# Early issue of expert weight pieces, and the first expert's gather made by channels in four parts, in a hybrid SSD, attention and mixture-of-experts layer

## The chip, the cores and the metric

One core of a Trainium2 chip runs the whole layer as one program, written engine by engine with semaphores. The metric is the device time of one execution in microseconds (us); the median of three runs is given before.

## What is computed

One decoder layer on 256 tokens of width 1024, in f32: a norm, one wide projection, a state space branch and a causal attention branch with forget gates, their gated merge; a cross attention to a memory of 256 rows; and a mixture of 32 experts, of which each token takes 4. All matrices are read from memory once. Cut to the part that the change is in:

```python
# h = h + cross_attention(...), 256 tokens x 1024
u = rms_norm(h, norm_ffn_g)
logits = u @ w_router + b_router                 # 32 experts
top_vals, top_idx = lax.top_k(logits, 4)
gates = softmax(top_vals)
# for each expert e, on the tokens x that chose it:
hgl = x @ w1[e] + b1[e]                          # 1024 -> 2048, 8 MiB of weights
glu = minimum(hgl[:, :1024], 7.0)
lin = clip(hgl[:, 1024:], -7.0, 7.0)
act = glu * sigmoid(1.702 * glu) * (lin + 1.0)
out[tokens] += gate * (act @ w2[e] + b2[e])      # 1024 -> 1024, 4 MiB of weights
```

## The kernel before

**The first half, to about 424 us,** is dense projections. Weights come in units of 256 columns (1 MiB each), which SP loads in the order of a list into two buffers (`load(u)`, L383). ScalarE rounds each to a high part (`w_hi`, L1205), VectorE makes the low part (`w_lo`, L1565), and TensorE makes three products of each (L648 to L650). The last units are `ck` and `cv` (keys and values of the cross attention), `cq`, and `co` (its output projection, `in_w_cross_o`). `load(u)` waits until the unit two before is split (L385).

**The experts, from 434.8 us,** use each expert's 12 MiB once. The working memory is an arena of 25 pages of 8 KiB per partition. Eleven slots of two pages each hold expert weights; a half piece `m` is 2 MiB, three pairs of them make an expert: two pairs of `w1`, by input channels, and one of `w2`. The first eleven halves go to slots that are still used by the first half's tensors (`W_AT`, L188): slot 3 lies on pages 6 and 7 (`kxT` and `Vx`, keys and values of the cross attention), slot 8 on pages 18 and 19 (the split memory rows, `B_`), slot 9 on pages 20 and 21 (`qx`, then squares). So SP brings them in quarters of 1 MiB, `piece(m, k)` (L388), each placed by hand in SP's order behind a wait for the tensor that it overwrites (L411 to L446). Halves 11 and 12 follow in quarters when the first expert's first products have been made (`first_page`, L458), and from 13 on each half waits for the release of the half that was in its slot (`e_free`, L346; L464 and L470). From the eighth expert to the thirtieth, both halves are loaded as one 4 MiB transfer (`whole`, L366).

SP has one instruction stream: a wait in it holds all that stands behind. TensorE, ScalarE, VectorE likewise run the order in which the code is written.

**The routing, 424 to 435 us.** TensorE makes the last logits and square sums, then turns `hT` (channels by tokens) to tokens by channels in PSUM with products by the identity (`by_token`, L862), and ScalarE copies four tiles of 128x512 to `xtok`, scaled by the token's norm (`tokens`, L1414). VectorE picks the four largest logits of each token and makes the mask `msk` (L1834). TensorE sums the mask over the tokens before each one (L918 to L920: a token's place in its expert's list) and counts each expert's tokens (L921, L922). VectorE makes from this `posm`, and from it the selection matrix `sel` of the first expert (`selection`, L1838: token by slot, 64 slots) and the counts of further items (L1863, L1864). `keep_clock` (L888) is one product of 128x256 of constants into an unused bank, once before these products and once behind them.

**The first expert's gather:** TensorE multiplies `sel` by `xtok`, all 1024 channels, the two halves of them side by side in the two halves of bank 2 (`gather(1)`, L955), 64 columns of weights and 512 moving ones. ScalarE copies the result in two parts (L1436), TensorE transposes it in four (`gathered_transposes`, L964), and VectorE scales it by the gains of the norm and writes `xgT`, channels by slots (L1868), in two parts. `weights_in` (L999) then multiplies `xgT`, 64 columns of weights at a time, by the expert's `w1`: four parts `(s, h)`, of half a piece each, in 16 instructions. Every later expert's gather and transposes are made while the one before it is at work (`item`, L1070), in the same way.

```python
gather(1)                       # waits for tok_ready 4: all four token tiles
offsets()                       # places of further items
bias(0); bias(1)
gathered_transposes(1)
```

## Time and profile before

| | |
|---|---|
| runs | 1341.42 us median of 3 (1339.36 to 1342.38) |
| the profiled execution | 1341.73 us, of which the span from first to last instruction is 1340.0 us |
| TensorE (PE) busy | 1295.9 us, 97% |
| VectorE (DVE) busy | 423.0 us, 32% |
| ScalarE (ACT) busy | 326.0 us, 24% |
| moved by DMA | 474.79 MB, 354 GB/s over the span |
| granted TensorE clock, mean | 0.989 |

The profile is one execution. Its views used here: the busy shares and the memory rate in 40 slices; the same by stretches (windows); who waited for whom (waits); the chain of work that ended last, followed back (chain); instructions in order of time (timeline); the DMA issues with their time from issue to landing; groups of instructions by line. An f32 product that is not a plain transpose shows as two instructions. PEld is TensorE's weight load, SPq the DMA issues of SP. Neighbouring instructions of one kind are merged: the second number is then the length of the group.

### The profile page before, as it was taken

To read this page: it belongs to the slowest core of one execution; us is meant where nothing else is said; L and a number is where in the kernel's file an instruction comes from. 1 tells how busy PE (TensorE), PEld (TensorE's weight loads), DVE (VectorE), ACT (ScalarE), POOL (GpSimd) and SP (SyncE) were. 2 spreads that over 40 slices of the span, in tenths; PEclk is the share of its full clock that TensorE was granted. 3 is DMA by queue.
4 is the path that set the end of the run, shared out by engine and by line. 5 is a ranking of instruction groups with operands and counts; after the bars stand their busy time and mean duration, and the time that the engine had idled before them with its cause. 6 is when DMAs were issued, how large, how long until landed. Compare 5 with 4: busy or idle time off the path is not lost.

```text
span 1340.0 us, 17338 instructions
## 1 busy us (share of the span) xinstructions
PE 1295.9 (97%) x7372; PEld 717.8 (54%) x7372; DVE 423.0 (32%) x803; ACT 326.0 (24%) x533; POOL 39.8 (3%) x66
## 2 busy tenths in 40 slices
PE   8999999999999999999999999999999999999997
PEld 7999999999998333333333333333333333333332
DVE  6765777586453212111121112111112111112111
ACT  5865456554443111000010001000001000000102
POOL 2002210001001000000000000000000000000000
PEclk9999999999999999999999999999999999999999
DMA  7566544559839999999999999999999999999996
GB/s 225 163 205 205 160 141 141 160 187 368 292 119 409 389 429 427 417 435 428 435 430 428 433 429 435 428 433 432 429 435 427 435 430 431 435 427 433 426 425 252
DMA packets 88930, 474.79 MB, mean 354 GB/s; under 512 B 7398, under 2 KB 68998, under 8 KB 70568
## 3 DMA queue, kind: packets, MB, share of 16 engines
q1 hardware_dynamic: 88176, 470.71, 86.6%
q10 hardware_dynamic: 696, 3.24, 0.7%
q8 instruction: 45, 0.74, 0.2%
q14 instruction: 13, 0.11, 0.0%
HBM read 472.86 MB, written 1.07 MB: 354 GB/s over the span
## 4 chain that ended last, share of the span: by engine, by line
PE 70%; DMA 24%; DVE 3%; ACT 1%; issue 0%; ACTq 0%; DVEq 0%
DMA arena<-in_w_expert_in 23%; PE ps L1014 21%; PE ps L1066 13%; PE ps L648 6%; PE ps L650 6%; PE ps L649 6%; PE ps L980 4%; PE ps L960 3%; DVE w_lo L1565 1%; PE ps L972 1%; PE ps L988 1%; DMA w_raw<-in_w_in 1%; PE ps L639 1%; PE ps L1042 1%; PE ps L640 1%; PE ps L641 1%
## 5 line engine op out<-in xcount | busy, mean ns | idle before, releaser
L1014 PE MATMUL ps<-arena 128*64 128x512 f32 x2048 | 462.1, 607 | 25.4 <-DMA arena<-in_w_expert_in 24.9
L1014 PEld LDWEIGHTS ps<-arena 128*64 128x64 f32 x2048 | 148.3, 140 | 331.5 <-issue 290.7
L1907 DVE TENSOR_SCALAR arena<-ps 128x512 f32<-128x512 f32 x32 | 22.1, 692 | 664.8 <-PE ps L1014 664.8
L1066 PE MATMUL ps<-arena 128*64 128x512 f32 x1024 | 227.0, 595 | 0.0
L648 PE MATMUL ps<-A_hi,w_hi 128*128 128x256 f32 x576 | 165.5, 287 | 2.9 <-DVE w_lo L1565 2.2
L1565 DVE TENSOR_TENSOR w_lo<-w_raw,w_hi 128x1024 fp32r<-128x1024 f32 x120 | 145.1, 1250 | 66.8 <-ACT w_hi L1205 66.5
L649 PE MATMUL ps<-A_lo,w_hi 128*128 128x256 f32 x576 | 162.9, 283 | 0.0
L650 PE MATMUL ps<-A_hi,w_lo 128*128 128x256 f32 x576 | 162.9, 283 | 0.0
L1066 PEld LDWEIGHTS ps<-arena 128*64 128x64 f32 x1024 | 70.6, 137 | 135.6 <-issue 135.5
L1442 ACT ACTIVATE arena<-arena 128x512 f32<-128x512 f32 x32 | 20.1, 629 | 479.0 <-DVE arena L1907 479.0
L1205 ACT ACTIVATE w_hi<-w_raw 128x1024 fp32r<-128x1024 f32 x120 | 120.1, 1048 | 36.6 <-DMA w_raw<-in_w_cross_o 6.8
L648 PEld LDWEIGHTS ps<-A_hi,w_hi 128*128 128x128 f32 x576 | 110.4, 192 | 5.4 <-issue 3.6
L649 PEld LDWEIGHTS ps<-A_lo,w_hi 128*128 128x128 f32 x576 | 110.4, 192 | 0.1
L650 PEld LDWEIGHTS ps<-A_hi,w_lo 128*128 128x128 f32 x576 | 110.4, 192 | 0.0
L1454 ACT ACTIVATE arena<-ps 128x512 f32<-128x512 f32 x32 | 19.1, 597 | 236.5 <-PE ps L1066 236.5
L980 PE MATMUL ps<-arena 64*128 64x512 f32 x264 | 65.6, 615 | 0.7 <-ACT arena L1454 0.7
L960 PE MATMUL ps<-arena,wrt 128*64 128x512 f32 x256 | 62.0, 605 | 0.1
L980 PEld LDWEIGHTS ps<-arena 64*128 64x128 f32 x264 | 22.7, 186 | 43.1 <-issue 41.5
L1849 DVE TENSOR_TENSOR arena<-ps,prm 128x512 f32<-128x512 f32 x31 | 21.4, 692 | 70.8 <-PE ps L972 70.8
L960 PEld LDWEIGHTS ps<-arena,wrt 128*64 128x64 f32 x256 | 15.5, 136 | 42.2 <-issue 41.8
L1432 ACT ACTIVATE arena<-ps 128x512 f32<-128x512 f32 x31 | 18.5, 597 | 75.3 <-PE ps L960 75.3
L648 PE MATMUL ps<-C_hi,w_hi 128*128 128x256 f32 x128 | 36.3, 284 | 0.4 <-DVE w_lo L1565 0.4
(309 smaller groups left out, 1274.8 us busy)
## 6 DMA issues: line engine op xcount, KB each, us to landing
arena<-in_w_expert_in SPq DMA_DIRECT2D x46, 4096.0 KB, 37.4
arena<-in_w_expert_out SPq DMA_DIRECT2D x23, 4096.0 KB, 39.4
arena<-in_w_expert_in SPq DMA_DIRECT2D x27, 2048.0 KB, 17.2
w_raw<-in_w_in SPq DMA_DIRECT2D x32, 1024.0 KB, 5.4
arena<-in_w_expert_out SPq DMA_DIRECT2D x10, 2048.0 KB, 15.1
arena<-in_w_expert_in SPq DMA_DIRECT2D x18, 1024.0 KB, 10.5
arena<-in_w_expert_out SPq DMA_DIRECT2D x16, 1024.0 KB, 20.8
w_raw<-in_w_cross_kv SPq DMA_DIRECT2D x8, 1024.0 KB, 7.6
```

Source lines behind the costliest of these rows:

```text
L648: mm(o, w_hi[:, s, k, :], a_hi[:, k, :], start=(k == 0), stop=False)
L649: mm(o, w_hi[:, s, k, :], a_lo[:, k, :], start=False, stop=False)
L650: last = mm(o, w_lo[:, s, k, :], a_hi[:, k, :], start=False, stop=(k == KT - 1))
L960: last = mm(ps[64 * half:64 * (half + 1), 2, :], sel[:, 64 * tb:64 * (tb + 1)], xtok[:, tb, 512 * half:512 * (half + 1)], start=(tb == 0), ...
L980: last = mm(ps[:, 4 + 2 * tb + half, :], sgT[rows, tb * P:(tb + 1) * P], ys[rows, :], start=False, stop=bool(each), skip_group_check=True)
L1014: last = mm(ps[64 * half:64 * (half + 1), b, :], xg_cols[:, 2 * h + c, s, :], columns[:, :, half, :], start=False, stop=(s + h + c == 3), ...
L1066: last = mm(ps[64 * half:64 * (half + 1), bank, :], cols[:, c, h, :], w[:, at:at + 512], start=(h + c == 0), stop=(h + c == 4))
L1205: A(w_hi[:, p % 4, :, :], raw_w[u % 2][:, :, j * P:(j + 1) * P], ACT.Copy).then_inc(w_hi_ready, 1)
L1442: A(sig, glu, ACT.Sigmoid, scale=ALPHA).then_inc(sig_ready, 1)
L1565: V_.tensor_tensor(w_lo[:, p % 4, :, :], raw_w[u % 2][:, :, j * P:(j + 1) * P], w_hi[:, p % 4, :, :].bitcast(f32), ALU.subtract).then_inc( ...
L1849: V_.tensor_tensor(xgT.rearrange("p (m a j) -> p m a j", m=4, a=2), ps[:, 2, :].rearrange("p (m a j) -> p m a j", m=4, a=2), prm[:, 136:14 ...
L1907: V_.tensor_scalar(glu, ps[:, 0, :], LIMIT, None, ALU.min).then_inc(glu_ready, 1)
```

## The change

Three edits.

1. SP's order. Quarter (9,0) (page 20, `qx`) and (3,0) (page 6, `kxT`) are issued as soon as the last scores of the cross attention are made (`x_psum`), then, when the last value projection is done (`w_done`), (8,0), the third `co` load, (8,1), the fourth `co` load; only (3,1) (page 7, `Vx`) still waits for the attention's outputs (`xo_psum`).
2. `keep_clock` and its two products are gone.
3. The first expert's gather is made by channels: `first_gather(part)` has the token tile (every fourth of 512 channels, 128 of them) as weights and `sel` as the moving operand, so that channels by slots come out directly, 2 groups of 128 channels a part. The copy on ScalarE and the transposes are gone for the first expert. VectorE scales each of the four parts by itself. Parts 0 and 1 are made before the bias, parts 2 and 3 between the first products of `weights_in`, as are the offsets. ScalarE copies the token tiles of the first 512 channels first. The semaphores' counts move with it.

```diff
--- before.py
+++ after.py
@@ -424,14 +424,16 @@
             piece(4, 1)
             for u in range(unit("cv", 3), unit("co", 2)):
                 load(u)
+            sp_.wait_ge(x_psum, X_H)
+            piece(9, 0)
+            piece(3, 0)
+            sp_.wait_ge(w_done, 2 * unit("cv", 3) + 2)
+            piece(8, 0)
+            load(unit("co", 2))
+            piece(8, 1)
+            load(unit("co", 3))
             sp_.wait_ge(xo_psum, X_H)
-            load(unit("co", 2))
-            piece(3, 0)
-            load(unit("co", 3))
             piece(3, 1)
-            piece(9, 0)
-            for k in range(2):
-                piece(8, k)
             sp_.wait_ge(w_lo_ready, 2 * (NU - 1))
             piece(6, 0)
             sp_.wait_ge(w_lo_ready, 2 * NU)
@@ -885,11 +887,6 @@
                 pe.wait_ge(dve_drained, drained(unit("co", 2))[1])
                 logits(2)
 
-            def keep_clock(bank, n):
-
-                for _ in range(n):
-                    mm(ps[:, bank, 0:S], idn, tri[:, 0:S], start=True, stop=True)
-
             def square_sums(chunks):
 
                 for c in chunks:
@@ -913,14 +910,12 @@
             square_sums((6, 7)).then_inc(ms_psum, 1)
             for c in range(2, 8):
                 by_token(c)
-            keep_clock(2, 1)
             pe.wait_ge(msk_ready, 1)
             mm(ps[:, 0, 0:NE], tri[:, 0:P], msk[:, 0, :], start=True, stop=True)
             mm(ps[:, 0, NE:2 * NE], tri[:, P:2 * P], msk[:, 0, :], start=True, stop=False)
             mm(ps[:, 0, NE:2 * NE], tri[:, 0:P], msk[:, 1, :], start=False, stop=True).then_inc(pos_psum, 1)
             mm(ps[0:NE, 3, 0:1], msk[:, 0, :], tri[:, P:P + 1], start=True, stop=False)
             mm(ps[0:NE, 3, 0:1], msk[:, 1, :], tri[:, P:P + 1], start=False, stop=True).then_inc(cnt_psum, 1)
-            keep_clock(2, 1)
 
             def offsets():
 
@@ -961,15 +956,20 @@
                                   xtok[:, tb, 512 * half:512 * (half + 1)], start=(tb == 0), stop=(tb == TB - 1))
                 last.then_inc(xg_psum, 1)
 
+            def first_gather(part):
+
+                s, h = part // 2, part % 2
+                for m in (2 * h, 2 * h + 1):
+                    at = 2 * P + SLOTS * (m % 2)
+                    for tb in range(TB):
+                        last = mm(ps[:, 2 + h, at:at + SLOTS], xtok[:, tb, 512 * s + m:512 * (s + 1):4],
+                                  sel[:, 64 * tb:64 * (tb + 1)], start=(tb == 0), stop=(tb == TB - 1))
+                last.then_inc(xgt_psum, 1)
+
             def gathered_transposes(i1):
-                first = type(i1) is int and i1 == 1
-                pe.wait_ge(xg_copied, i1 + (0 if first else 1))
+                pe.wait_ge(xg_copied, i1 - 1)
                 for m in range(4):
-                    if first and m == 2:
-                        last.then_inc(xgt_psum, 1)
-                        pe.wait_ge(xg_copied, 2)
-                    bank, at = (3, 2 * P + m * P) if first and m < 2 else (2, m * P)
-                    last = nc.tensor.transpose(ps[:, bank, at:at + P], xgs[:, m:512:4], idn)
+                    last = nc.tensor.transpose(ps[:, 2, m * P:(m + 1) * P], xgs[:, m:512:4], idn)
                 last.then_inc(xgt_psum, 1)
 
             def scatter(each=None):
@@ -987,23 +987,25 @@
 
                 mm(ps[:, b, :], selb[:, :], b1p[:, b, :], start=True, stop=False, skip_group_check=True)
 
-            pe.wait_ge(tok_ready, 4)
-            gather(1)
-            offsets()
+            pe.wait_ge(sel_ready, 2)
+            pe.wait_ge(tok_ready, 2)
+            first_gather(0)
+            pe.wait_ge(extra_ready, 1)
+            first_gather(1)
             pe.wait_ge(b1_ready, 2)
             pe.wait_ge(selb_ready, 1)
             for b in range(2):
                 bias(b)
-            gathered_transposes(1)
 
             def weights_in(i, parts):
 
                 first = type(i) is int and i == 0
-                pe.wait_ge(xgt_ready, i + (1 if first else 2))
+                if not first:
+                    pe.wait_ge(xgt_ready, i + 4)
                 for s in range(2):
                     for h in range(2):
-                        if first and (s, h) == (0, 1):
-                            pe.wait_ge(xgt_ready, 2)
+                        if first:
+                            pe.wait_ge(xgt_ready, 2 * s + h + 1)
                         w, loaded = parts[2 * s + h]
                         if loaded:
                             pe.wait_ge(*loaded)
@@ -1016,6 +1018,11 @@
                             if type(i) is int and (i, s, c) == (0, 0, 0):
                                 last.then_inc(first_page, 1)
                         last.then_inc(h_psum if s + h == 2 else e_used, 1)
+                        if first and s == 0:
+                            pe.wait_ge(tok_ready, 4)
+                            if h:
+                                offsets()
+                            first_gather(2 + h)
                         if type(i) is int and i == TABLES_AT:
                             if (s, h) == (0, 1):
                                 pe.wait_ge(y_ready, i + 1)
@@ -1411,9 +1418,10 @@
                 pair_square("co", n)
             root(3)
 
-            def tokens(tb):
-                for half in range(2):
-                    act.wait_ge(tok_psum, 2 * half + 2)
+            def tokens(half):
+
+                for tb in range(TB):
+                    act.wait_ge(tok_psum, 4 if half or tb else 2)
                     A(xtok[:, tb, 512 * half:512 * (half + 1)], ps[:, 4 + 2 * tb + half, :], ACT.Copy,
                       scale=st[:, tb:tb + 1]).then_inc(tok_ready, 1)
 
@@ -1424,16 +1432,10 @@
             for tb in range(TB):
                 A(em[:, tb, :], lg[:, tb, :], ACT.Exp, bias=smal[:, tb, 0:1]).then_inc(ex_ready, 1)
 
-            def gathered_half(row, q):
-                return row.rearrange("p (j m) -> p j m", m=4)[:, :, 2 * q:2 * q + 2]
-
             def gathered_copy(i1):
-                act.wait_ge(xg_psum, i1)
+                act.wait_ge(xg_psum, i1 - 1)
                 A(xgs, ps[:, 2, :], ACT.Copy).then_inc(xg_copied, 1)
 
-            act.wait_ge(xg_psum, 1)
-            for q in range(2):
-                A(gathered_half(xgs, q), gathered_half(ps[:, 2, :], q), ACT.Copy).then_inc(xg_copied, 1)
             act.wait_ge(meta_ready, 1)
             n_items = act.value_load(meta[0:1, NI:NI + 1], min_val=NE, max_val=MAX_ITEMS)
 
@@ -1845,7 +1847,7 @@
                 V_.tensor_scalar(selb[:, :], halves[:, :], pe1x[:, bass.ds(i, 1)], None, ALU.mult).then_inc(selb_ready, 1)
 
             def gathered_columns(i1):
-                dve.wait_ge(xgt_psum, i1 + 1)
+                dve.wait_ge(xgt_psum, i1 + 3)
                 V_.tensor_tensor(xgT.rearrange("p (m a j) -> p m a j", m=4, a=2),
                                  ps[:, 2, :].rearrange("p (m a j) -> p m a j", m=4, a=2),
                                  prm[:, 136:144].rearrange("p (m a) -> p m a", m=4).unsqueeze(3).to_broadcast([P, 4, 2, SLOTS]),
@@ -1863,11 +1865,13 @@
             link(V_.tensor_copy(ec[:, 0:1], ps[0:NE, 3, 0:1]))
             V_.scalar_tensor_tensor(out=ec[:, 4:4 + MAX_EXTRA], in0=fulls[:, :], scalar=ec[:, 0:1], in1=tri[0:NE, P:P + MAX_EXTRA],
                                     op0=ALU.is_lt, op1=ALU.mult, accum_out=ec[:, 1:2]).then_inc(extra_ready, 1)
-            for q in range(2):
-                dve.wait_ge(xgt_psum, q + 1)
-                V_.tensor_tensor(xgT[:, q * S:(q + 1) * S].rearrange("p (m a j) -> p m a j", m=2, a=2),
-                                 ps[:, 3 - q, S:2 * S].rearrange("p (m a j) -> p m a j", m=2, a=2),
-                                 prm[:, 136 + 4 * q:140 + 4 * q].rearrange("p (m a) -> p m a", m=2).unsqueeze(3).to_broadcast([P, 2, 2, SLOTS]),
+            for part in range(4):
+                s, h = part // 2, part % 2
+                two = slice(2 * h, 2 * h + 2)
+                dve.wait_ge(xgt_psum, part + 1)
+                V_.tensor_tensor(xgT.rearrange("p (m a j) -> p m a j", m=4, a=2)[:, two, s, :],
+                                 ps[:, 2 + h, 2 * P:2 * P + 2 * SLOTS].rearrange("p (m j) -> p m j", m=2),
+                                 prm[:, 136:144].rearrange("p (m a) -> p m a", m=4)[:, two, s].unsqueeze(2).to_broadcast([P, 2, SLOTS]),
                                  ALU.mult).then_inc(xgt_ready, 1)
             dve.wait_ge(extra_ready, 1)
             dve.wait_ge(off_psum, 1)
@@ -1897,7 +1901,8 @@
             n_items = dve.value_load(meta[0:1, NI:NI + 1], min_val=NE, max_val=MAX_ITEMS)
 
             def item(i):
-                dve.wait_ge(xg_psum, i + 1)
+                if not (type(i) is int and i == 0):
+                    dve.wait_ge(xg_psum, i)
                 selection(i + 1, i + 2)
                 for tb in range(TB):
                     V_.tensor_scalar(sg[:, P * tb:P * (tb + 1)], islot[:, :, :].rearrange("p a b -> p (a b)"),
```

**SP's queue around the last loads of the first half.** Rows are DMA issues in order; `w_raw<-in_w_cross_o` is a load of a `co` unit, `arena<-` an expert piece of 128 rows. Before:

```order
L386 DMA w_raw<-in_w_cross_o 128x8x256 x3
L391 DMA arena<-in_w_expert_in 128x2048
L386 DMA w_raw<-in_w_cross_o 128x8x256
L391 DMA arena<-in_w_expert_in 128x2048 x6
L391 DMA arena<-in_w_expert_out 128x2048 x2
L391 DMA arena<-in_w_expert_in 128x2048 x3
```

Now:

```order
L386 DMA w_raw<-in_w_cross_o 128x8x256 x2
L391 DMA arena<-in_w_expert_in 128x2048 x3
L386 DMA w_raw<-in_w_cross_o 128x8x256
L391 DMA arena<-in_w_expert_in 128x2048
L386 DMA w_raw<-in_w_cross_o 128x8x256
L391 DMA arena<-in_w_expert_in 128x2048 x3
```

Three pieces now stand ahead of the third `co` load and a fourth ahead of the last one; three pieces of `w1`, not six, follow the last load before the two of `w2`.

**TensorE from the last token products to the first expert's input products.** Rows are products as the program has them, f32 ones once. Before:

```order
L865 MATMUL ps<-ident,arena 128x128 x12
L891 MATMUL ps<-tri,ident 128x256
L918 MATMUL ps<-tab,tri 128x32
L919 MATMUL ps<-tab,tri 128x32
L920 MATMUL ps<-tab,tri 128x32
L921 MATMUL ps<-tri,tab 32x1
L922 MATMUL ps<-tri,tab 32x1
L891 MATMUL ps<-tri,ident 128x256
L960 MATMUL ps<-arena,wrt 64x512 x4
L928 MATMUL ps<-ec,tri 32x1
L929 MATMUL ps<-ec,tri 1x1
L988 MATMUL ps<-b1p,selb 128x512 x2
```

Behind them stand four transposes (L972) and then all 32 products of L1014 together. Now (`sel` shows as `wrt`, the token rows as `arena`):

```order
L918 MATMUL ps<-tri,tab 32x1
L965 MATMUL ps<-wrt,arena 128x64 x8
L988 MATMUL ps<-b1p,selb 128x512 x2
L1016 MATMUL ps<-arena 64x512 x8
L965 MATMUL ps<-wrt,arena 128x64 x4
L1016 MATMUL ps<-arena 64x512 x8
L923 MATMUL ps<-ec,tri 32x1
L924 MATMUL ps<-ec,tri 1x1
L965 MATMUL ps<-wrt,arena 128x64 x4
L1016 MATMUL ps<-arena 64x512 x16
```

The two products of constants (L891) are gone, sixteen products of 128x64 (L965) take the place of four of 64x512 and four transposes, and half of them and the offsets stand among the expert's own products.

## Rows read from the trace of the kernel before

**Rows 1.** What memory delivered, GB/s in 40 equal slices of the span

```profile
GB/s 225 163 205 205 160 141 141 160 187 368 292 119 409 389 429 427 417 435 428 435 430 428 433 429 435 428 433 432 429 435 427 435 430 431 435 427 433 426 425 252
```

**Rows 2.** Windows: us, PE, PEld, DVE, ACT, POOL busy (count), PEclk, DMA share, GB/s

```profile
380.00:400.00 20.00, 19.21 (x136) 18.07 (x135) 9.97 (x15) 8.47 (x15) 0.00 (x0) 1.00 0.18 57
900.00:1000.00 100.00, 94.01 (x422) 32.49 (x420) 13.20 (x30) 8.60 (x16) 0.00 (x0) 0.97 1.01 433
```

**Rows 3.** Waits from 815 to 1262 us: us in total, times, longest

```profile
PE ps L1014 <- DMA arena<-in_w_expert_in: 24.9, 15, 2.3
```

**Rows 4.** The chain that ended last, 1160 us to the end: start, length, what

```profile
1221.88 36.59 DMA arena<-in_w_expert_in
...
1258.51 8.78 PE ps L1014 x32
```

**Rows 5.** Windows, the same columns as before, two short stretches

```profile
389.00:398.00 9.00, 8.21 (x57) 7.59 (x56) 4.53 (x7) 3.57 (x7) 0.00 (x0) 1.00 0.00 0
458.00:462.00 4.00, 4.00 (x22) 1.42 (x20) 0.00 (x0) 0.34 (x1) 0.00 (x0) 1.00 0.85 303
```

**Rows 6.** Timeline, SP's DMA issues from 380 to 440 us: start, length

```profile
383.32 15.50 SPq L386 DMA_DIRECT2D w_raw<-in_w_cross_o  x2
398.86 0.58 SPq L391 DMA_DIRECT2D arena<-in_w_expert_in  x1
...
402.83 11.23 SPq L391 DMA_DIRECT2D arena<-in_w_expert_in  x6
...
436.79 2.04 SPq L391 DMA_DIRECT2D arena<-in_w_expert_out  x2
```

**Rows 7.** DMA issues at 383.32, 398.45, 445 to 449 and 458.21: KB, us to landing

```profile
w_raw<-in_w_cross_o SPq DMA_DIRECT2D x1, 1024.0 KB, 5.0
...
w_raw<-in_w_cross_o SPq DMA_DIRECT2D x1, 1024.0 KB, 4.9
...
arena<-in_w_expert_in SPq DMA_DIRECT2D x2, 2048.0 KB, 10.7
...
arena<-in_w_expert_in SPq DMA_DIRECT2D x1, 2048.0 KB, 8.2
```

**Rows 8.** The chain from 424 to 476 us: start, length, what

```profile
424.76 0.92 PE ps L858 x8
...
426.55 2.80 PE ps L865 x24
...
429.37 1.85 ACT arena L1417 x3
...
431.26 1.94 PE ps L960 x8
...
433.40 0.67 PE ps L988 x2
...
434.81 13.95 PE ps L1014 x64
...
461.61 13.73 PE ps L1014 x64
```

**Rows 9.** Timeline, TensorE at 429.60

```profile
429.60 0.30 PE L918 MATMUL ps<-tab,tri 128*128 128x32 f32 x2
```

**Rows 10.** Timeline, VectorE: slot selection, and the gate rows of the first expert

```profile
430.65 0.42 DVE L1841 TENSOR_SCALAR wrt<-islot,tab 128x64 f32<-128x64 f32 x2
...
439.31 0.59 DVE L1903 TENSOR_SCALAR arena<-islot,tab 128x128 f32<-128x128 f32 x2
```

**Rows 11.** Groups by line, 400 to 424 us: TensorE's weight loads of L858

```profile
L858 PEld LDWEIGHTS ps<-wrt,arena 128*128 128x128 f32 x8 | 1.0, 192 | 0.0
```

**Rows 12.** The clock: timeline and windows, TensorE

```profile
623.47 3.69 PE L1147 MATMUL ps<-tab 32*128 32x512 f32 x8
...
627.90:631.10 3.20, 3.20 (x10) 0.96 (x8) 0.00 (x0) 0.00 (x0) 0.00 (x0) 0.50 1.12 481
...
1171.08 7.09 PE L1014 MATMUL ps<-arena 128*64 128x512 f32 x32 [2.33 <-DMA arena<-in_w_expert_in]
```

## The prediction, made before the changed kernel was run

> **What bounds the kernel now.** I read the profile from the whole to the small. What memory delivered in 40 slices of 33.5 us [rows 1] shows the full rate from the thirteenth (402 us) on, 389 GB/s and more, and a hole just before, 119. In numbers [rows 2]: 57 GB/s at 380 to 400 us, 433 GB/s at 900 to 1000, where TensorE is busy for 94 of 100 us. So after 400 us two things are full at once. Which of them sets the end is told by the waits: from 815 to 1262 us TensorE waits only for expert weights, 24.9 us in 15 waits [rows 3]. The chain of waits closes it: a weight transfer that was issued at 1221.88 lands 36.6 us later, and from 1258.51 on TensorE works through to the end without a wait for memory [rows 4]. **The time is therefore the landing of that transfer plus some 81 us.** The transfers before it stand in one unbroken queue, so the landing moves only if the DMA engines were idle less somewhere before.
>
> Where were they idle? First at 389 to 398 us, with nothing moved at all [rows 5]: after the issue at 383.32 the queue has none for 15 us, until 398.45, and then many [rows 6]. That hole is what the first part of the change fills. There is a second place: 458 to 462 us, with 303 GB/s [rows 5]. There the queue ran out, since every issue from 436.79 us on is a refill, made when TensorE lets go of a page. The refill of 458.21 landed after only 8.2 us, the two before it after 10.7 [rows 7], and the one of 1221.88 after 36.6: the queue grows, because TensorE uses an expert in 26.6 us (input products end at 448.76 and 475.34 [rows 8]) and memory needs 29.1 us, 12.58 MB by 433 GB/s. From 466 us on the queue never runs dry.
>
> **Part 1, early pieces.** Four pieces of 1 MiB, (9,0), (3,0), (8,0) and (8,1), are issued at about 387 to 394 us instead of 398.9 for (3,0) and from 402.8 on for the others [rows 6], each as its page comes free (scores done, last value projection done). They fill the hole. Two loads of cross_o weights stand behind them in the queue, and these have readers. The first, now issued by its split at about 394 and not at 398.45, has some 2 MiB ahead of it and lands near 401; before it landed 4.9 us after its issue, at 403.3 [rows 7]. ScalarE splits it when it lands, and its products have to wait for those of the two column blocks before it anyway. So it costs nothing, with 2 us of cover ahead of the split. The second is still issued at about 402.4, when its buffer is split, with only (8,1) still under way before it, and cannot come later than it did. The waits placed before the pieces hold up SP alone, and what is queued behind them has no earlier chance.
>
> What it brings is not the hole's 10 us. By 436.8 us all first fillings have been issued either way, and after that a page must be given back first. With an empty queue, a refill lands after its own time: 1 MiB took 5.0 us when nothing else ran (issue at 383.32) and 4.9 (398.45) [rows 7], of which 1.05 MB by 433 GB/s is 2.4, so 2.5 us are fixed, and 2 MiB take 2.5 + 4.8 = 7.3. The refill of 458.21 then lands at 465.5 and not at 466.4, **0.9 us earlier**, and everything behind it in the queue by as much. The rows allow 0.8 to 1.0. This bounds the gain: 0.9 us, less whatever TensorE is later at that point. Below nothing it cannot go by this part alone. The Trainium skill, DMA: Bandwidth & Descriptors, Anatomy of one DMA, fits 2.0 us plus bytes by 436 GB/s, for transfers that GpSimd issues. An estimate by it is 6.8 us for 2 MiB, a gain of 1.4 us, and a sum 0.5 us lower than mine; its 4.4 us for 1 MiB is under the 4.9 and 5.0 of the rows, which decide.
>
> **Parts 2 and 3, gather and clock products: how late is TensorE at 448.8 us?** The path before [rows 8, 9]: token products end at 429.35, a clock product delays the prefix products to 429.60, ScalarE's last token tile ends at 431.22, then come the gather of 1.94 us from 431.26, offsets, bias of 0.67 from 433.40, transposes, the scaling on VectorE, and 13.95 us of expert products from 434.81, to 448.76.
>
> Now, step by step. The prefix products follow the token products directly, 0.23 us earlier; the slot selection on VectorE, at 430.65 with 0.42 us [rows 10], ends at 430.84. Two token tiles are done by then, since ScalarE makes the last three in 1.85 us from 429.37 on. The second clock product stood beside VectorE's selection, while TensorE waited, and is off the path. First gather product: 430.9, against 431.26. A part of the gather is 4 products of 128 rows by 64 columns, 8 instructions. None of this form is in the trace. The nearest rows are L858 (32 columns, 8 in 0.92 us) and L865 (128 columns, 24 in 2.80) [rows 8]: 0.115 and 0.117 us an instruction. I take 0.115, 0.92 us a part. From above it is bounded by a weight load of 192 ns [rows 11], which lies beside the product before it there, if the stride of four elements stops that: 1.54 us a part. From below I allow a fifth less than any row, 0.09 and 0.72 us, since the nearest rows bound no form with another stride. Two parts: 432.75. Bias 0.67: 433.4. The two scalings wait for nothing that TensorE needs later. The first expert product starts at 433.45, **1.4 us earlier**. But two parts (1.84) and the offsets (0.2, what lay between gather and bias) now stand among the products, which themselves are 13.73 us, as in the second expert [rows 8]: 433.45 + 13.73 + 2.04 = 449.2. **So TensorE is 0.45 us later** at the end of the first expert's input products, and at the refills of 445.4 us on: 32 gather instructions (3.7 us) are more than the old gather, the four transposes, the clock product on the path and the waits (about 3.2 together). The bounds of this term are -0.35 at 0.72 us a part and +2.9 at 1.54. The ScalarE copies taken away lie on the old path and are counted in its 434.81.
>
> What is late next: VectorE now does four scalings before the expert table, the last at about 442.5. Its chain from there to the gate rows ended at 439.9 [rows 10], 5 us after the scalings, and will end near 447.5; the first reader, the second expert's gather, comes after the products and the scatter, near 451. Cover 3 us. ScalarE's count of items, released by the same chain, likewise has no reader before the first activation at about 449.
>
> **Sum.** 0.9 gained, 0.45 given back: -0.45 us. The profiled execution, 1341.73 us (span 1340.0), would be 1341.3; it lies 0.3 over the median of the runs, 1341.42, from which I forecast **1341.0 us**. 0.2%, 2.7 us, is about what a measurement of this kernel can tell from no change; this is far inside it.
>
> **Rivals.**
> *A, the hole counts in full.* The four pieces, 4.19 MB, are 9.7 us of DMA time at 433 GB/s: 1331.7. For it: the DMA engines are full from 400 to 1280 us. Against: each refill hangs on a page, and the queue is seen near empty at 458. Chance 0.06.
> *B, the clock.* At 2.4 GHz 32 expert instructions take 7.09 us, with a stretch at 1.2 GHz in them 8.78, 1.7 us more [rows 4, 12]. The stretch in the closing chain follows a wait for weights; another, at 627.9, follows no wait but 3.7 us of products with 32 rows [rows 12]. So thin work can bring the clock down here, and the change takes two full products out of such a stretch, leaves a gap of some 0.6 us at 430.2 and puts thin products there. A fall in the first expert makes TensorE 0.45 + 1.7 late, less 0.9: +1.2, 1342.7. Slower by over 0.2% takes a lateness of 3.6 us: two stretches, 1344.4. Against: the clock is whole at 389 to 398 us, though TensorE was busy for only 8.2 of these 9 us [rows 5]. The Trainium skill, TensorE: Matmul & The Clock Gate, Part 1, says that the slow state is the default and only activity lifts it, which speaks against taking the products out. One stretch 0.12, two 0.05.
> *C, weight loads bound the gather* (1.54 us a part): 2.9 - 0.9, 1343.4. Chance 0.08; with one stretch of B it is slower.
> *D, the last stretch at 1.2 GHz, right after 1258.51, is missed,* as after the wait of 2.33 us that ended at 1171.08, where 32 instructions took 7.09 us [rows 12]: it lies on the closing chain, 1.7 us, 1339.3. Chance 0.10. It hangs on where the stretches fall, not on the change.
> *E, the early pieces come no earlier,* because SP is held by its waits: then only the 0.45 us late counts while the queue has slack, 1341.5 to 1341.9. Chance 0.05.
>
> **How the numbers follow.** The forecast has the remaining 0.54. The three runs span 3.0 us, so I add about 1 us to each side of the cases: low 1338.7 (D and the spread), high 1343.6 (B with one stretch, C). This leaves out A, two stretches and some tails. Faster by over 0.2%: A, part of D, the tails, 0.16. Slower: two stretches, C with one, the tails, 0.11. Within: 0.73.
>
> **What the profile after would show.** Right: over 100 GB/s at 390 to 398 us and gaps before 436; the first refill at about 435.1 and not 436.8; the refill of 458 issued some 0.4 us later and landed after 7.2 to 7.5 us; 8 gather instructions in 0.9 us; the weight landing of 1258.5 half a microsecond earlier. Wrong if gather parts take over 1.2 us, if the granted clock falls between 430 and 450, if the refill of 458 still takes over 8 us, or if TensorE waits for cross_o weights.

## The result and the profile after

The change made the kernel slower: 1347.09 us, the median of six runs (1346.08 to 1350.94), against 1341.3 before (1339.32 to 1342.38, six runs), a ratio of 1.0048, 95% interval 1.0037 to 1.0058. That lies above the forecast range, which ended at 1343.6. The profiled execution took 1346.91 us, with a span of 1345.1, 5.1 over before.

First what memory delivered, in the 40 slices of the page after:

```profile
GB/s 226 160 207 202 160 144 136 169 190 371 287 237 296 312 429 427 421 432 428 434 430 430 431 435 428 432 435 431 431 434 432 432 432 435 428 432 433 424 426 261
```

Beside [rows 1], the hole of 119 in the twelfth slice is a 237, and the two slices behind it have fallen from 409 and 389 to 296 and 312. In windows of the kernel after (us, then PE, PEld, DVE, ACT and POOL busy, PEclk, DMA share, GB/s):

```profile
380.00:400.00 20.00, 19.22 (x135) 18.07 (x135) 9.93 (x15) 8.48 (x15) 0.00 (x0) 1.00 0.72 257
410.00:426.00 16.00, 16.00 (x141) 15.46 (x140) 5.27 (x5) 4.21 (x6) 4.11 (x5) 1.00 0.55 196
900.00:1000.00 100.00, 95.17 (x434) 32.98 (x430) 13.48 (x32) 8.60 (x16) 0.00 (x0) 0.98 1.00 433
```

380 to 400 us went from 57 to 257 GB/s [rows 2], which is 4.0 MB more. Nearly as much, 3.6 MB, is then missing at 410 to 426, where the kernel before had:

```profile
410.00:426.00 16.00, 16.00 (x141) 15.46 (x139) 4.39 (x5) 5.13 (x7) 4.81 (x5) 1.00 1.01 422
```

The rate of the long stretch is the same 433. SP's issues on the timeline of the kernel after show that the early pieces came when they should:

```profile
387.19 6.51 SPq L391 DMA_DIRECT2D arena<-in_w_expert_in  x3
393.75 0.43 SPq L386 DMA_DIRECT2D w_raw<-in_w_cross_o  x1
394.22 0.58 SPq L391 DMA_DIRECT2D arena<-in_w_expert_in  x1
402.27 0.38 SPq L386 DMA_DIRECT2D w_raw<-in_w_cross_o  x1
```

So the time was lost elsewhere. The chain of waits of the kernel after, from 426 us on (start, length, what):

```profile
426.38 2.80 PE ps L867 x24
429.20 1.27 ACT arena L1425 x2
430.52 4.00 PE ps L965 x16
434.52 0.96 PE ps L988 x2
435.48 4.66 PE ps L1016 x16
440.13 2.01 PE ps L965 x8
442.14 3.58 PE ps L1016 x16
...
445.92 2.01 PE ps L965 x8
447.93 7.02 PE ps L1016 x32
454.95 1.92 PE ps L980 x8
...
467.80 13.73 PE ps L1016 x64
```

L965 is the four-part gather. A part, 8 instructions, takes 2.0 us, and the 16 of the first two parts 4.00. The first expert's input products end at 454.95, and ended at 448.76 before [rows 8]. Two things more are to be seen: the first 16 products take 4.66 us and the next 16 only 3.58, and the bias (L988) took 0.67 before and takes 0.96. The windows of the kernel after on both sides of 434.2 us say why:

```profile
430.50:434.15 3.65, 3.63 (x16) 3.63 (x16) 0.73 (x5) 2.36 (x4) 0.00 (x0) 1.00 1.01 426
434.20:437.60 3.40, 3.40 (x10) 1.32 (x11) 0.29 (x1) 0.00 (x0) 0.00 (x0) 0.50 0.57 227
```

Right behind the gather the granted clock is 0.50, the lower of its two levels, 1.2 GHz instead of 2.4, for 3.4 us. In the first window the column of weight loads (PEld) is as full as that of the products, 3.63 of 3.65 us: in the gather TensorE is bound by its weight loads. The groups by line of the kernel after, 424 to 455 us (the last figure ahead of the bar's end is the mean in ns):

```profile
L965 PE MATMUL ps<-wrt,arena 128*128 128x64 f32 x32 | 8.2, 403 | 0.6 <-ACT arena L1425 0.6
L965 PEld LDWEIGHTS ps<-wrt,arena 128*128 128x128 f32 x32 | 7.7, 327 | 1.5 <-issue 0.8 <-DVE wrt L1843 0.6
L867 PEld LDWEIGHTS ps<-ident,arena 128*128 128x128 f32 x25 | 3.0, 192 | 0.0
```

A load of the gather takes 327 ns, one of the same 128 by 128 shape with neighbouring columns 192. Last, the refill that was issued at 458.21 before, and the closing of the chain. The refill's line in the timeline of after, and the answer on the transfers issued from 464 to 465 us (KB, us to landing):

```profile
464.40 0.33 SPq L472 DMA_DIRECT2D arena<-in_w_expert_in  x1
```

```profile
arena<-in_w_expert_in SPq DMA_DIRECT2D x1, 2048.0 KB, 7.2
```

and the chain of after from 1200 us on:

```profile
1226.93 36.80 DMA arena<-in_w_expert_in
...
1263.77 8.70 PE ps L1016 x32
```

The refill is issued 6.2 us later and lands 7.2 us after its issue instead of 8.2, so 5.2 us later. The landing that sets the end comes at 1263.7 instead of 1258.5 [rows 4], later by the same 5.2. The waits from 815 to 1290 us have hardly changed (us in total, times, longest), beside [rows 3]:

```profile
PE ps L1016 <- DMA arena<-in_w_expert_in: 25.3, 15, 2.5
```

Nothing was lost after the first expert. Both TensorE and the queue run as before, 5 us later.

### The profile page after: what moved, and what is told of

Read it like the earlier page. It is cut to its first block, busy times and chain, and to the rows that moved or that the text cites. A ratio compares the mean times of both kernels' runs of the same rounds, so it can differ in the third digit from the quotient of the medians.

```text
span 1345.1 us, 17368 instructions
## 1 busy us (share of the span) xinstructions
PE 1300.9 (97%) x7388; PEld 724.3 (54%) x7388; DVE 424.4 (32%) x805; ACT 325.9 (24%) x531; POOL 38.9 (3%) x66
## 4 chain that ended last, share of the span: by engine, by line
PE 73%; DMA 23%; DVE 2%; ACT 1%; issue 0%; ACTq 0%; DVEq 0%
DMA arena<-in_w_expert_in 22%; PE ps L1016 21%; PE ps L1073 13%; PE ps L650 7%; PE ps L651 7%; PE ps L652 7%; PE ps L980 4%; PE ps L955 3%; PE ps L988 1%; DVE w_lo L1567 1%; PE ps L972 1%; DMA w_raw<-in_w_in 1%; PE ps L641 1%; PE ps L1049 1%; PE ps L642 1%; PE ps L643 1%
## 5 line engine op out<-in xcount | busy, mean ns | idle before, releaser
L1851 DVE TENSOR_TENSOR arena<-ps,prm 128x512 f32<-128x512 f32 x31 | 21.4, 691 | 70.8 <-PE ps L972 70.8
L650 PE MATMUL ps<-B_hi,w_hi 128*128 128x256 f32 x128 | 36.6, 286 | 0.0
```

The costliest lines, as they stand in the source:

```text
L650: mm(o, w_hi[:, s, k, :], a_hi[:, k, :], start=(k == 0), stop=False)
L1851: V_.tensor_tensor(xgT.rearrange("p (m a j) -> p m a j", m=4, a=2), ps[:, 2, :].rearrange("p (m a j) -> p m a j", m=4, a=2), prm[:, 136:14 ...
```

## The experiments

Twelve kernels were run, each timed beside the kernel before on the same chip. Profiled executions differ by up to 3.7 us in where the routing begins, with the same work ahead of it. So I count from S, the start of ScalarE's last run of token tiles, at most 0.04 us behind TensorE's last token product in every kernel (429.37 before [rows 8], 429.20 after). "Refill" is the one of 458.21 before: its issue and its landing, both counted from S. "Closing landing" is that of the transfer that sets the end, 1258.5 before. The last column is the timed ratio, less one, times 1341 us, with its 95% interval.

| kernel | S | refill: issue - S | refill: landing - S | closing landing - S | timed against before, us |
|---|---|---|---|---|---|
| before | 429.37 | 28.8 | 37.1 | 829.1 | |
| 1 early pieces alone | 430.04 | 28.9 | 36.8 | 828.0 | +0.7 (-0.7 to 2.0) |
| 4 no clock products alone | 429.12 | 28.9 | 38.5 | 828.0 | +0.9 (-0.4 to 2.3) |
| 2 neighbouring columns | 430.77 | 29.8 | 37.1 | 829.1 | 0.0 (-1.5 to 1.3) |
| 9 two channels apart | 432.30 | 29.9 | 37.2 | 829.2 | +1.5 (-0.1 to 3.1) |
| 11 permuted tiles, wait filled | 428.76 | 30.4 | 37.6 | 829.6 | -0.3 (-2.0 to 1.5) |
| 6 permuted tiles | 428.69 | 31.4 | 38.6 | 830.8 | -0.7 (-1.7 to 0.5) |
| 10 stride of four in two parts | 428.61 | 31.7 | 38.9 | 830.9 | +1.6 (0 to 3.2) |
| 8 delayed, new order of transfers | 428.67 | 31.9 | 39.8 | 831.1 | +3.5 (2.1 to 4.7) |
| 7 delayed, old order | 430.76 | 31.9 | 40.1 | 832.1 | +3.1 (1.7 to 4.4) |
| after | 429.20 | 35.2 | 42.4 | 834.5 | +6.4 (5.0 to 7.8) |
| 5 gather without early pieces | 429.34 | 36.0 | 43.3 | 835.4 | +6.0 (4.3 to 7.9) |
| 12 stride of four, wait filled | 429.06 | 36.8 | 44.0 | 835.8 | +5.6 (3.9 to 7.5) |
| 3 clock products back | 429.42 | 36.9 | 44.2 | 836.2 | +7.0 (5.2 to 8.6) |

The times follow the landing of this one refill, within the intervals, but for kernel 6. Its profiled execution had a fall of the clock (below) that its timed ones need not all have.

Two things limit what one profiled execution tells. First, the closing landing is as much later than before as the refill's, to 0.2 us, except in 1, 4 and 8, where it comes 0.8, 2.5 and 0.7 us earlier than the refill would give. The cause is open. Second, the last stretch at 1.2 GHz, which rival D has missing: the 32 products behind the closing landing took 8.70 or 8.78 us, with a stretch at 1.2 GHz, before, after and in 3, 5, 8, 10, 11 and 12, but 7.09 at the full clock in 1, 2, 4, 6, 7 and 9. These 1.7 us come on top, and make the spans of these six shorter.

**1. The early pieces alone.** The kernel before with SP's issues in the order of the change (the first hunk of its diff, nothing else).

> The kernel before with the new order of SP's issues and nothing else. In the changed kernel the refill that was issued at 464.4 us landed 7.2 us later, on an empty queue, and the end moved by 5.1 us while TensorE was 6.2 us later at that place. Theory of the refills: TensorE's times to 458 us stay, the refill of 458.2 lands after 7.2 us and not 8.2, and the end comes 0.9 to 1.0 us earlier: ratio 0.9993. Rival, the hole counts in full: 9.7 us earlier, 0.9928. Rival, the early pieces cost something in the queue or in memory: no gain or a loss, refill still 8 us.

Measured: 1341.57 us, ratio 1.0005 (0.9995 to 1.0015). The window of 410 to 426 us of this kernel shows where the bytes are missing once the hole is filled (before: 422 GB/s):

```profile
410.00:426.00 16.00, 16.00 (x141) 15.46 (x139) 5.46 (x5) 3.51 (x6) 4.10 (x5) 1.00 0.55 201
```

The refill was issued at 458.89 and landed 7.9 us later, not 7.3. The rival that counts the hole in full is refuted. The gain of 0.9 us doesn't show in the time either. The refill landed 0.3 sooner from S. The closing landing came 1.1 sooner, but it did so in experiment 4 too, which has no early pieces.

**2. Neighbouring columns.** The change with the stationary operand of the gather taken from 128 neighbouring channels, which gives the first expert its channels in another order.

```
-  xtok[:, tb, 512 * s + m:512 * (s + 1):4]
+  xtok[:, tb, 512 * s + P * m:512 * s + P * (m + 1)]
```

> The changed kernel, but the first expert's gather takes 128 neighbouring columns of the token rows as weights in place of every fourth of 512. The channels are then in the wrong order for the first expert, so that its part of the output is not the reference's; the work is otherwise the same. Theory of the stride: a part of the gather (8 instructions) takes 0.92 us and not 2.0, the weight load 192 ns and not 327, and TensorE reaches the refills of the first expert 4.3 us sooner, so 4.3 us less than the changed kernel: 1342.8 with a stretch at 1.2 GHz in the first expert, 1341.1 without. Rival, the form (64 moving columns, or the selection matrix as moving operand): parts stay at 2.0 us and the time at 1347.

Measured: 1340.77 us, ratio 1.0000 (0.9989 to 1.001). The whole loss is gone with this one edit. Its chain:

```profile
432.10 2.00 PE ps L965 x16
434.09 0.52 PE ps L988 x2
434.62 3.58 PE ps L1016 x16
438.20 1.04 PE ps L965 x8
```

and its weight loads, in the groups by line:

```profile
L965 PEld LDWEIGHTS ps<-wrt,arena 128*128 128x128 f32 x32 | 3.8, 191 | 1.5 <-issue 0.8 <-DVE wrt L1843 0.6
```

A part costs 1.0 us and a load 191 ns. The clock stayed whole through the routing.

**3. The clock products back.** The change with both products of constants where they were before.

> The changed kernel with the two products of constants put back in their old places. Theory A, the fall of the clock at 434.2 us comes from their absence: the granted clock stays whole there, and the time is 1.7 us less, near 1345.4. Theory B, the 4 us of slow gather products with 64 moving columns bring the clock down: it falls all the same at 434 to 436 us, and the time is 0.2 to 0.5 us more than the changed kernel's.

Measured: 1348.64 us, ratio 1.0052 (1.0039 to 1.0064). The clock fell all the same, at 433.9 us, and the first 16 input products took 5.88 us in the chain. The stretch is twice as long as in the change, 6.8 us:

```profile
433.90:440.70 6.80, 6.80 (x20) 2.99 (x21) 0.29 (x1) 0.00 (x0) 0.00 (x0) 0.50 0.36 145
```

So the missing products of constants are not why it fell. Theory B holds for the clock. It gave a time 0.2 to 0.5 us over that of the change. The median is 1.5 over, by the timed ratios it is 0.5.

**4. No clock products, nothing else.** The kernel before without the two.

> The kernel before without its two products of constants and nothing else changed. Theory A, they hold the clock up: it falls near 430 to 435 us, TensorE is 1.2 to 1.7 us late in the first expert, and the time is 0.5 to 1 us more than before, 1342. Theory B, they do nothing: no fall, the routing 0.2 to 0.3 us shorter, the time the same or 0.2 less, since memory has the queue to make up.

Measured: 1342.66 us, ratio 1.0007 (0.9997 to 1.0017), and no fall of the clock in the routing. The old gather starts 1.9 us from S with and without these products, so neither stood on the path, where the prediction had counted one. The refill landed 9.6 us after its issue in the profiled execution. I have no cause for that. It didn't pass to the end: the closing landing came 1.1 us sooner from S than before.

**5. The gather without the early pieces.** The change with SP's old order.

> The change with the transfers of the routing in their old order: only the four-part gather and the missing clock products are left. Theory A (the time goes to TensorE's lateness alone, and the early pieces are worth nothing while the first expert ends late): same end of the first expert's input products as in the change (6.0 to 6.4 us later than before), the refill behind it lands 7.2 to 7.5 us after its issue, time 1346.5 to 1347.5 us. Theory B (the early pieces cost something while TensorE is late, for instance by leaving less for the gaps that follow): 1345 us or less. Theory C (they pay, because the hole before the routing is filled): 1348.5 us or more.

Measured: 1347.56 us, ratio 1.0045 (1.0032 to 1.0059). That is 0.06 over the range of theory A, whose mechanism holds. With the strided gather the early pieces are worth as little as without it, as far as the times tell. TensorE's input products ended 7.2 us later than before, from S, and not 6.0 to 6.4, since here too the clock was down for 6.8 us, from 432.5 on. And its refill landed 7.3 us after the issue, though nothing was brought forward:

```profile
465.34 0.33 SPq L470 DMA_DIRECT2D arena<-in_w_expert_in  x1
```

```profile
arena<-in_w_expert_in SPq DMA_DIRECT2D x1, 2048.0 KB, 7.3
```

The short landing thus comes with the four-part gather and not with the early pieces.

**6. Permuted token tiles.** The change with ScalarE writing each token tile in the order of the channels' residue of four. The gather then loads neighbouring columns and computes what the change computes.

```
-  A(xtok[:, tb, 512 * half:512 * (half + 1)], ps[:, 4 + 2 * tb + half, :], ...
+  A(xtok[:, tb, 512 * half:512 * (half + 1)].rearrange("p (m j) -> p m j", m=4),
+    ps[:, 4 + 2 * tb + half, :].rearrange("p (j m) -> p m j", m=4), ...
```

> The change with ScalarE writing the token tiles with the channels in the order of their residue of four, so that every stationary operand of the gather is 128 neighbouring columns. Its output is the change's. Theory A (the stride of four in the weight load is the whole of the price): a gather part of 8 products takes 0.92 to 1.1 us, no fall of TensorE's clock in the routing, the input products of the first expert end about 1.0 us later than before, time 1340.5 to 1341.5 us, as the forecast had it. Theory B (writing the tiles permuted moves the price to ScalarE, whose writes now have the stride): ScalarE's copies take 1.2 us instead of 0.6 each, the gather begins 1 us or more later, time 1342 to 1343.5 us. Weight loads of 192 ns and 0.115 us an instruction under A.

Measured: 1340.57 us, ratio 0.9995 (0.9987 to 1.0004). ScalarE's two copies ahead of the gather take the 1.27 us that they take in the change, so reading PSUM four elements apart costs nothing there (it is the reads that have the stride, and not the writes, as I had expected), and theory B is refuted. The transposes of every later expert take neighbouring columns here as well. Its chain:

```profile
428.69 1.27 ACT arena L1425 x2
...
430.01 2.00 PE ps L965 x16
432.01 0.69 PE ps L988 x2
432.70 5.04 PE ps L1016 x16
437.74 1.04 PE ps L965 x8
```

The price of the gather is as expected. The clock isn't: it fell here too, in the profiled execution, at 432.2 us, and the first products took 5.04 instead of 3.58 us. That is half of theory A refuted. The time nevertheless came out as expected. In the profiled execution the 1.7 us of later landing and the 1.7 of the missing stretch behind the closing landing cancel.

**7 and 8. A plain delay.** The kernel before (7), and the kernel of experiment 1 (8), with seven products of constants ahead of the first expert's bias.

```
             pe.wait_ge(selb_ready, 1)
+            keep_clock(0, 7)
             for b in range(2):
                 bias(b)
```

> The kernel before with seven products of constants of 128x256 (406 ns each by the trace) ahead of the first expert's bias: TensorE 3.0 us later from there, at the full clock and with no new kind of weight load. Theory A (lateness of the first expert passes to the end in full once its refill finds the queue empty, less the 1.0 us that the refill then lands sooner): end of the input products +3.0, refill lands 7.2 to 7.5 us after issue, time 1343.0 to 1344.0 us. Theory B (there is slack in front of the closing stretch that takes up such a delay): 1341.0 to 1342.3 us. Theory C (every us counts): 1344.3 us or more.

> The same seven products of constants, with the transfers of the routing in the order of the change. Theory A (the early pieces only move idle time of the queue from before the routing to within it): the same time as the delayed kernel with the old order, within 0.5 us, that is 1343.0 to 1344.0 us. Theory B (the early pieces make the kernel more sensitive to a late TensorE, since less is left to move while it is waited for): 1344.5 us or more. Theory C (they take up a part of the delay): 1342.5 us or less.

Measured: 1344.36 us, ratio 1.0023 (1.0013 to 1.0033) with the old order, and 1344.41, ratio 1.0026 (1.0016 to 1.0035), with the new one. The delay in the chain of the first is 3.2 us, and the refill comes 3.0 later from S in both:

```profile
434.79 3.22 PE ps L891 x14
438.01 0.47 PE ps L988 x2
```

By theory A the two were to take 1343.0 to 1344.0. The first is in the range of theory C, every us counts, and the second between the ranges of A and B. The pair is 0.05 apart, as theory A of the second had it. So a late first expert passes to the end without a strided load and without a fall of the clock. What fell is my reason for the discount of 1.0 us: with the old order the refill still took 8.2 us. The refill before it explains this. Issued at 453.22, it took 12.3 us, the second line, and so was still under way at 462.62:

```profile
453.22 0.33 SPq L470 DMA_DIRECT2D arena<-in_w_expert_in  x1
```

```profile
arena<-in_w_expert_in SPq DMA_DIRECT2D x1, 2048.0 KB, 12.3
```

In the kernel after, that earlier refill was issued at 454.99 and landed at 463.69, ahead of the issue at 464.40. There the seven issues behind 437 us are spread over 25.9 us (438.46 to 464.40), since gather parts stand among the products that free the pages. Before and in the delayed kernel they take 21.4 (436.79 to 458.21, 441.20 to 462.62).

**9. Two channels apart.** The gather's stationary columns with a stride of two.

> The change with the stationary operands of the four-part gather taken two channels apart instead of four (other channels, so another result; the shapes and counts are the same). Theory A (the time of a weight load grows with the distance between its columns): a load between 192 and 327 ns, a part of 8 products between 1.03 and 2.01 us, time 1342 to 1345.5 us. Theory B (any distance over one costs the full price): 327 ns and 2.0 us a part, 1346.5 to 1347.5 us. Theory C (two apart is read as fast as neighbours): 192 ns, 1.03 us a part, 1340.3 to 1342.3 us.

Measured: 1343.47 us, ratio 1.0011 (0.9999 to 1.0023). The load's mean is 196 ns, and a part takes 1.09 us:

```profile
L965 PEld LDWEIGHTS ps<-wrt,arena 128*128 128x128 f32 x32 | 4.0, 196 | 1.5 <-issue 0.8 <-DVE wrt L1843 0.6
```

Theory C holds for the load: two apart is read nearly as fast as neighbours, four apart is not. The median lies 1.2 us above what C gave, with an interval that touches its range; from S the refill landed only 0.1 us after that of before.

**10. A stride of four in two parts.** Parts 0 and 1 of the gather with neighbouring columns (which leaves these channels in another order), parts 2 and 3 as in the change.

> The change with neighbouring columns in parts 0 and 1 of the gather and the stride of four kept in parts 2 and 3, which stand among the products with the expert's weights. Theory A (each strided part costs its 1.0 us wherever it stands, and adds to the end in full): parts 2.0 us for the first two together and 2.0 us for each of the others; against the kernel with neighbouring columns everywhere +2.0 us, so 1342.5 to 1343.5 us, and up to 1.6 us more if TensorE's clock falls here too. Theory B (loads of parts 2 and 3 hide beside the products around them): 1340.5 to 1341.5 us. The fall of the clock may come with neighbouring columns too (it was seen in one such run and not in the other), so it is read apart.

Measured: 1342.67 us, ratio 1.0012 (1.0000 to 1.0024). In its chain the strided part lies in full between the expert's products, 2.01 us against 1.04 in experiment 2, and nothing hides it:

```profile
429.92 2.00 PE ps L965 x16
...
432.44 3.58 PE ps L1016 x16
436.03 2.01 PE ps L965 x8
438.04 3.58 PE ps L1016 x16
```

The refill was issued 1.9 us later than in experiment 2, from S, and the clock stayed whole.

**11 and 12. TensorE's wait filled.** Three products of constants ahead of the gather, in the kernel of experiment 6 (11) and in that of experiment 3 (12). The wait turned out to be shorter than the 1.3 us that I had taken. TensorE was idle for 0.55 us there in experiment 6 and not at all in 3, so the three products also delay the gather.

```
+            keep_clock(2, 3)
             pe.wait_ge(sel_ready, 2)
             pe.wait_ge(tok_ready, 2)
             first_gather(0)
```

> The change with the permuted token tiles, and three products of constants (128x256) in the 1.3 us in which TensorE waits for ScalarE ahead of the gather. Theory A (TensorE's clock falls behind the four-part gather because of this idle time ahead of it; without it the clock holds): no stretch at 0.5 between 425 and 450 us, first input products 3.5 us instead of 5.0, end of the input products 0.9 to 1.1 us later than before, measured from ScalarE's copies, time 1339.0 to 1340.0 us, faster than both kernels. Theory B (the fall comes from the gather with its 64 moving columns itself): the clock falls as before, 1340.5 to 1341.2 us. Theory C (the constants delay the gather by what they take): 1341.5 us or more.

> The change with both products of constants back and three more of them in TensorE's wait ahead of the gather; the gather keeps its stride of four. Theory A (the idle time brings the clock down): no fall here either, time 1.6 us under the change, 1345.0 to 1346.0 us. Theory B (the strided gather brings it down): the clock falls at 433 to 435 us as in the change, 1346.5 to 1348.5 us.

Measured: 1341.31 us, ratio 0.9998 (0.9985 to 1.0011), and 1347.28 us, ratio 1.0042 (1.0029 to 1.0056). With neighbouring columns the clock held and the first products took 3.58 us, yet the kernel was no faster than before, where theory A gave 1339.0 to 1340.0. The gather began 2.3 us from S instead of 1.3, so 0.9 of what the clock gave back went to the delay, which is a part of what theory C expected. With the stride of four it fell again, though TensorE had not been idle at all from 424 us on, and its gather began 1.3 us later than in experiment 3. The window of experiment 12:

```profile
436.40:439.70 3.30, 3.30 (x10) 0.92 (x8) 0.00 (x0) 0.00 (x0) 0.00 (x0) 0.50 0.02 7
```

So idle time ahead of the gather isn't what brings the clock down with the stride of four. Experiment 3 says the same: its chain is TensorE's own work without a gap from 424 us to the fall. Counted over the profiled executions, the clock fell in all four with four strided parts (after, 3, 5, 12), in none of the five with the old gather (before, 1, 4, 7, 8), and in one of five with parts of neighbouring columns or a stride of two (6, not 2, 9, 10, 11). With one execution of each, this is a count and no proof that the stride causes the fall. What decides it in the last group stays open. No kernel tried is measurably faster than before. Experiment 6 is as fast, and computes the same.

## Why the prediction was wrong

**The step that failed is the term for the gather: "I take 0.115, 0.92 us a part".** A part took 2.0 us in the change and 1.0 with neighbouring columns. Four parts are then 8.0 us and not 3.7: 4.3 us of the error. The prediction had named a part of over 1.2 us and a fall of the clock between 430 and 450 as signs of being wrong, and both showed. The upper bound failed as well. It took the 192 ns of an unstrided load [rows 11] for the worst case, where loads hide behind nothing, 1.54 us a part. The loads in fact became longer, 327 ns. The prediction said that the nearest rows "bound no form with another stride", and it then reasoned from below only. A strided form did stand in the trace of before: the transposes of every later expert load columns four apart. The groups by line of the kernel before, 452 to 700 us, and of experiment 6, where the same line has neighbouring columns:

```profile
L972 PEld LDWEIGHTS ps<-ident,arena 128*128 128x128 f32 x36 | 5.0, 209 | 0.3
```

```profile
L972 PEld LDWEIGHTS ps<-ident,arena 128*128 128x128 f32 x36 | 3.8, 140 | 0.3
```

The first of these was there to be read, and 209 ns is over the bound of 192. It wouldn't have given 327, but it was a warning that the stride has a price.

**Rival B, the clock, came true together with C.** They had 0.12 and 0.08, and the text said that the two together are slower. One stretch of 3.4 us at 1.2 GHz cost 1.5 us here (bias 0.96 against 0.52, first products 4.66 against 3.58 in experiment 2), where B had 1.7. In 3 and 5 it was 6.8 us, at a cost of 2.7 and 2.3. Of B's three reasons two are refuted: neither the missing products (3, 4) nor the gap (3, 12) is needed for the fall with the stride. The third, thin products in that place, is left. The two cases were weighed as if they were independent. The strided loads make the long gather, and the fall came with them in all four kernels that had them in every part.

The sum from S: the input products ended 25.75 us after S instead of 19.39, 6.4 later. Of this, 5.8 are the two terms above, 0.45 was in the forecast, and 0.1 is left. 6.4 less the 1.0 of the refill's shorter landing is 5.4, and the end came 5.1 later (spans), 6.4 by the timed ratio, 5.0 at its lower end.

**The 0.9 us of part 1 was the right size and the wrong cause.** The refill did land 7.2 us after its issue. But the early pieces give only 7.9 in both kernels that have them without the new gather (1, 8), and the new gather gives 7.3 without them (5). The three pairs that differ by the early pieces alone (before and 1, after and 5, 7 and 8) have medians 0.5 us or less apart. What the queue holds at 458 us is set by how fast the first expert hands back pages, and only by some 0.3 us by what was loaded before 436. Against this stands that the closing landing was 0.9 to 1.1 us sooner with the early pieces in each pair. After against 5 the longer fall of the clock in 5 explains it, and 4 reached the same without early pieces, so their worth is not shown to be nothing, only too small for these times.

**What held.** The time hangs on the landing of that refill and what follows it, and lateness there passes to the end in full (7, 8). The early pieces were issued at 387 to 394 us, the second load of cross_o at 402.27, and TensorE waited for neither. VectorE's later table was covered: its last gate row starts at 452.49 us and takes 0.6, and the first gather that reads it starts at 456.87. Rival A is refuted (1), and so is E, since the pieces were early. D did not come in the profiled execution of the change (8.70 us), but did in six of the twelve others, which is more than its 0.10. The first refill at 438.46, not at 435.1, and the late closing landing are the missed gather again.

The Trainium skill, TensorE: Matmul & The Clock Gate, LDWEIGHTS (loading the stationary operand), has the time of a load depend on its number of columns alone. These traces disagree: with 128 columns each time it was 191 ns for neighbours, 196 two apart and 327 four apart.

## What to carry to other kernels

A new access pattern of an operand is a new instruction: price it by a row with the same stride, search the whole trace for one, and where there is none set no upper bound from rows without it. When the end hangs on a queue that is refilled as pages are handed back, find the first hand-back behind which the queue never runs dry again; work that delays it costs in full, and transfers that are only moved from one idle stretch ahead of it to another brought nothing that the times could show. Rivals that share a cause belong in one case with one chance.

## What was not expected of the hardware

- A stationary float32 operand of 128 by 128 with its columns four elements apart loads in 327 ns against 191 for neighbours, and one instruction of a stream then takes 0.25 us against 0.13. Two apart costs 5 ns.
- The same stride costs 69 ns in the loads of transposes (209 against 140), half of the 136 in those of products.
- ScalarE reads a tile from PSUM four elements apart in the time that it takes for neighbours (1.27 us for two).
- TensorE's clock can fall while it is busy without a gap: in experiment 12 at 436.4 us, 0.7 us after 3.57 us of gather products bound by their strided loads. In the kernel with neighbouring columns and the same gap-free start (11) it held.
- The clock doesn't change the time of a strided load. In experiment 5 it fell in the middle of the gather, at 432.5 us. The loads took 326 ns ahead of it (the first line, 430.66 to 432.4 us) and 329 behind it (the second, 432.7 to 434.6). Loads of neighbouring columns, 192 ns at the full clock, took 321 and 324 in the bias at half of it (after, 5). So the fall costs nothing as long as strided loads set the pace: the first two parts took 3.99 us in 5 and 4.00 in the change.

```profile
L963 PEld LDWEIGHTS ps<-wrt,arena 128*128 128x128 f32 x8 | 1.9, 326 | 0.6 <-DVE wrt L1841 0.6
L963 PEld LDWEIGHTS ps<-wrt,arena 128*128 128x128 f32 x8 | 2.0, 329 | 0.0
```
